# A scan's 64x64 chunk inverse: from full-width blocks to compressed blocks, two heads in one matmul

## The reference, cut to what matters

```
def step(S, inp):
    d_t, k_t, v_t, kk_t, a_t = inp[:5]
    sa = jnp.einsum("bhvk,bhk->bhv", S, -kk_t)
    S = (S * d_t[:, :, None, :] + sa[..., None] * (kk_t * a_t)[:, :, None, :]
         + v_t[..., None] * k_t[:, :, None, :])
    out = jnp.einsum("bhvk,bhk->bhv", S, inp[5]) if emit else None
    return S, out
```

## Time and profile before

| | us |
|---|---|
| median of 3 runs (2806.54 to 2811.82) | 2809.04 |
| the profiled execution, span | 2808.7 |
| time of the profiled execution outside its span, as far as the profile shows | none |
| scan, from about 1071 to 1757 | 686 |
| thirteen middle units of the scan (1179.5 to 1692) | 512.5 |

### The profile page before, as it was taken

One profiled execution on the slowest core, in us unless ns is written; L12 is line 12 of the kernel. 1 busy time (PEld: TensorE's weight loads), 2 busy tenths in 40 slices (PEclk: granted clock), 3 DMA queues, 4 the chain that ended last, 5 costly groups with the idle time before them and its releaser, 6 DMA issues. The chain is left out here.

```text
span 2808.7 us, 66348 instructions
## 1 busy us (share of the span) xinstructions
PE 2512.4 (89%) x28704; PEld 1935.4 (69%) x28704; DVE 1519.4 (54%) x2491; ACT 1099.4 (39%) x1771; POOL 735.1 (26%) x422
## 2 busy tenths in 40 slices
PE   7998899999889995888888887889999999898997
PEld 5776577777667784777777776768788655475666
DVE  4744589863652213556666663344542466525975
ACT  4633321152453433455545543334422344323133
POOL 2422301422212225555545551100000000032132
PEclk9999999999899996999999999989999999998998
DMA  4224344434335531111111100633522100044431
GB/s 159 83 68 135 128 135 124 122 105 162 116 125 183 201 122 59 43 43 55 38 54 54 32 15 26 240 129 103 159 79 86 57 0 1 11 173 139 137 109 68
DMA packets 90286, 272.63 MB, mean 97 GB/s; under 512 B 13584, under 2 KB 14608, under 8 KB 89872
## 3 DMA queue, kind: packets, MB, share of 16 engines
q1 hardware_dynamic: 73104, 229.25, 25.6%
q10 hardware_dynamic: 16896, 39.16, 4.0%
HBM read 203.01 MB, written 36.70 MB: 85 GB/s over the span
## 5 line engine op out<-in xcount | busy, mean ns | idle before, releaser
L375 PE MATMUL ps<-h_parts_conv,w_parts_one 128*128 128x512 f32 x3168 | 579.8, 343 | 16.9 <-DVE h_parts_conv L361 13.7
L375 PEld LDWEIGHTS ps<-h_parts_conv,w_parts_one 128*128 128x128 f32 x3168 | 492.4, 190 | 107.5 <-issue 24.1
L375 PE MATMUL ps<-scratch_scan 64*64 64x64 f32 (+1 forms) x16704 | 383.1, 234 | 96.2 <-issue 56.1
L375 PEld LDWEIGHTS ps<-scratch_scan 64*64 64x64 f32 x16704 | 345.9, 137 | 139.5 <-issue 105.8
L372 ACT ACTIVATE scratch_scan<-ps 128x384 f32<-128x384 f32 x560 | 238.4, 495 | 331.7 <-PE ps L375 180.3
L443 POOL TENSOR_TENSOR w_parts_one<-ring,w_parts_one 128x1024 fp32r<-128x1024 f32 x83 | 208.2, 2509 | 581.4 <-ACT w_parts_one L372 581.3
L375 PE MATMUL ps<-h_parts_attn,w_parts_rwkv_out 128*128 128x512 f32 (+1 forms) x1536 | 329.2, 373 | 4.6 <-DVE h_parts_attn L369 4.6
L375 PEld LDWEIGHTS ps<-h_parts_attn,w_parts_rwkv_out 128*128 128x128 f32 x1536 | 263.2, 189 | 64.0 <-issue 9.4
L443 POOL TENSOR_TENSOR w_parts_rwkv_out<-ring,w_parts_rwkv_out 128x1024 fp32r<-128x1024 f32 x31 | 74.6, 2409 | 812.5 <-ACT w_parts_rwkv_out L372 812.5
L369 DVE SCALAR_TENSOR_TENSOR scratch_conv<-scratch_conv,vec 128x512 f32<-128x512 f32 (+1 forms) x408 | 252.6, 691 | 0.2
L372 ACT ACTIVATE w_parts_rwkv_out<-ring 128x1024 fp32r<-128x1024 f32 x104 | 109.5, 1056 | 344.0 <-PE ps L375 325.8
(11 more groups left out here) (219 smaller groups left out, 3263.6 us busy)
## 6 DMA issues: line engine op xcount, KB each, us to landing
ring<-in_weights SPq DMA_DIRECT2D x311, 512.0 KB, 3.7
rwkv_spill<-scratch_conv ACTq DMA_DIRECT2D x64, 384.0 KB, 2.3
stream<-rwkv_spill SPq DMA_DIRECT2D x64, 384.0 KB, 3.6
scratch_conv<-scratch_conv SPq DMA_DIRECT2D x120, 103.1 KB, 2.2
scratch_conv<-scratch_conv SPq DMA_DIRECT2D x120, 67.4 KB, 2.0
x_spill<-stream ACTq DMA_DIRECT2D x16, 384.0 KB, 2.5
kept_gate<-scratch_attn ACTq DMA_DIRECT2D x64, 64.0 KB, 2.6
y_spill<-scratch_scan SPq DMA_DIRECT2D x8, 384.0 KB, 2.5
```

The source lines that it names most:

```text
L375: return nc.tensor.matmul(o, l, r, start=start, stop=stop)
```

## The change

P is now held compressed: before level n (block size b = 2^n) each row of a matrix keeps only the b columns of its own diagonal block, which stand in the first b of 64 columns of `PQ[(n - 1) % 2]`.
- There are six levels, `n` = 0 to 5. Level 0 needs no product with a P: `first_t` is six matmuls, each with a 128x128 stationary N (both heads and both halves) and a constant of four columns, `first_q` two matmuls with an identity. `first_inverse`, `p_start`, `p_diagonal` and the transposes PI are gone; a sixth transposition P6 of the whole inverse is there.
- `inv_t` is 12 matmuls (two heads side by side as 128 stationary columns, 64 rows), with 2b moving columns. `inv_q` is 12 matmuls (both heads as 128 stationary rows, 64 columns), with 2b moving columns from `TZ`, whose other half is zero.
- `t_copy` copies 12b elements for each half of the partitions.
- ScalarE writes the old P, times a row mask, into the two half blocks of the next size (`other_half`: two copies of 384 elements at n = 1 to 4, one at n = 0 and 5); VectorE adds Q to one of them (`inverse_update`, one operation of 384).
- The transposes P1 to P5 leave PSUM through VectorE, times a block mask (`turned_inverse`, two operations of 384 each); P6 goes through ScalarE (`full_turned`). The transposed k (`k_turned`) moves from VectorE to ScalarE.
- GpSimd masks N in one operation of 768 elements for each level.

TensorE's order of one phase becomes: T(1), WU, Q(1), WU, P2, BT, MR, T(2), NP, Q(2), MR, chain 1, P3, KT, chain 2, T(3), G, chain 3, Q(3), G, chain 4, AV, P4, VT, KS, chain 5, T(4), G, chain 6, Q(4), chain 7, RC, BO, P5, chain 8, T(5), AT, chain 9, `first_t` (for w1), Q(5), RS, chain 10, `first_q`, P6, outputs, P1 (for w1). On VectorE the new `inverse_update(w1, 0)` stands behind `cumulate`, and `turned_inverse(w1, 1)` is the last operation of the phase, behind `finish_out`, `normal_out` and `add_output`. On ScalarE `other_half(w2, n + 1)` stands right behind the copies that follow T(n). GpSimd's order is masks 2 and 3, `scaled_k`, mask 4, `bonus_add`, mask 5, `grown_k`, `grown_b`, `bonus_weights`, then masks 0 and 1 of w1.

```
-        NLV = 5
+        NLV = 6
...
-        T1, MT, NE = (take(NSTEP, CH) for _ in range(3))
+        MT, NE = (take(NSTEP, CH) for _ in range(2))
+        TZ, TZ0 = take(2, HALFC * CH), take(2, NSTEP)
...
+        def own(n, t):
+            b = inner(n)
+            return t.rearrange("p g (o b) -> p g o b", o=1).broadcast_to([P, NSTEP, max(CH // (2 * b), 1), b])
+
+        def half_of(n, side):
+            return PQ[n % 2].rearrange("p g (k s b) -> p g k s b", s=2, b=inner(n))[:, :, :, side, :]
...
+        def inverse_ready(engine, w, n):
+            if n == 1:
+                engine.wait_ge(*read_at("Q0", w, 0))
+            else:
+                engine.wait_ge(added, added_at(w, n - 1))
+            engine.wait_ge(halved, halved_at(w, n - 1))
...
-            def first_inverse(w):
...
+            def first_t(w):
+                pe.wait_ge(n_masked, masked_at(w, 0))
+                room_for(pe, "T0", w, 0)
+                first = fill_bank("T0", w, 0) * 512
+                o = PS[:, first:first + 2 * NSTEP].rearrange("p (x j y) -> p j y x", x=2, y=2)
+                ones = C("own_half").rearrange("p (y x) -> p y x", y=2)
+                for j in range(HALFC):
+                    last = mm(o[:, j, :, :], NT[0][:, 2 * j:2 * j + 2, :].rearrange("p h t -> p (h t)"), ones)
+                last.then_inc(*done_inc("T0", w, 0))
+
+            def first_q(w):
+                pe.wait_ge(*read_at("T0", w, 0))
...
+                for par in range(2):
+                    o = PS[HS[par], first:first + NSTEP].rearrange("p (j x) -> p x j", x=2)
+                    last = mm(o, C("ident2"), TZ0.rearrange("p x (j y) -> p y x j", y=2)[:, par])
+                last.then_inc(*done_inc("Q0", w, 0))
+
+            def inv_t(w, n):
+                pe.wait_ge(n_masked, masked_at(w, n))
+                inverse_ready(pe, w, n)
+                b = inner(n)
                 for j in range(HALFC):
                     for par in range(2):
...
+                        last = mm(PS[:, par * 512 + 2 * b * j:par * 512 + 2 * b * (j + 1)].rearrange("p (x b) -> p x b", x=2),
+                                  NT[n % 2][HS[par], 2 * j:2 * j + 2, :].rearrange("p h t -> p (h t)"), PQ[(n - 1) % 2][HS[par], 2 * j:2 * j + 2, 0:b])
+                        if j == HALFC - 1:
+                            last.then_inc(t_done, 1)
+
+            def inv_q(w, n):
+                pe.wait_ge(t_copied, 2 * product_at(w, n))
                 for e in range(2):
-                    pe.wait_ge(*read_at(f"P{lv}" if lv else "PI", w, e))
+                    pe.wait_ge(*read_at(f"P{n}", w, e))
...
                     for par in range(2):
-                        for h in range(2):
-                            last = mm(bank3(h)[HS[par], j, :], PT[w % 2][HS[h], 2 * j + par, :], T1[HS[h], 2 * j + par, :])
-                            if (j, par) == (HALFC - 1, 1):
-                                last.then_inc(q_done, 1)
+                        last = mm(PS[HS[par], 2 * b * j:2 * b * (j + 1)].rearrange("p (x b) -> p x b", x=2), PT[w % 2][:, 2 * j + par, :], t[:, par, j])
+                last.then_inc(q_done, 1)
...
+            def inverse_update(w, n):
...
+                    if n < NLV - 1:
+                        v.wait_ge(halved, halved_at(w, n))
+                        vtt(into, into, own(n, q), ALU.add).then_inc(added, 1)
                     else:
...
+                        stt(into[:, :, 0], PQ[(n - 1) % 2][:, :, 0:b], keep, q, ALU.mult, ALU.add).then_inc(added, 1)
...
+            def turned_inverse(w, n):
+                for e in range(2):
+                    v.wait_ge(*done_at(f"P{n}", w, e))
+                    vtt(blocks(n, PT[w % 2][:, half(e), :]), blocks(n, bank3(fill_bank(f"P{n}", w, e))), own_block(n)).then_inc(*read_inc(f"P{n}", w, e))
...
+            def t_copy(w, n):
+                a.wait_ge(t_done, 2 * product_at(w, n))
+                b = inner(n)
+                t = PS[:, 0:1024].rearrange("p (y z) -> p y z", y=2)[:, :, 0:NSTEP * b].rearrange("p y (j x b) -> p x y j b", x=2, b=b)
+                for h in range(2):
+                    act(TZ[HS[h], h, 0:NSTEP * b].rearrange("p (y j b) -> p y j b", y=2, b=b), t[HS[h], h], ACT.Copy).then_inc(t_copied, 1)
...
+            def other_half(w, n):
...
+                    before = own(n, PQ[(n - 1) % 2][:, :, 0:inner(n)])
+                    if n < NLV - 1:
+                        act(half_of(n, d), before, ACT.Copy, scale=keep).then_inc(halved, 1)
+                    act(into, before, ACT.Copy, scale=by).then_inc(halved, 1)
...
+            def off_blocks(w, n):
...
+                nc.gpsimd.tensor_tensor(NT[n % 2].rearrange("p (j s) t -> p j s t", s=2), XX[:, aa_plane(w), :, 0, :, :], level_mask(n),
+                                        ALU.mult).then_inc(n_masked, 1)
```

More of the change, by code:

```diff
@@ L83, in constants @@
     m = [((s // (2 * b) == t // (2 * b)) & (s // b != t // b))[:, :64] for b in (1, 2, 4, 8, 16, 32)]
-    m = [m[0] & (t < s)[:, :64], m[0] & (t > s)[:, :64], *m[1:]]
     put("inv_mask", np.concatenate(m, 1))
+    row, block = s[:, :1], np.arange(64)[None]
+    put("own_block", np.concatenate([row // 2 == block // 2, row // 4 == block // 4]
+                                    + [row // b == block[:, :64 // b] for b in (8, 16, 32)], 1))
+    put("even_rows", np.concatenate([row // b % 2 == 0 for b in (1, 2, 4, 8, 16, 32)], 1))
+    put("odd_rows", np.concatenate([row // b % 2 == 1 for b in (1, 2, 4, 8, 16, 32)], 1))
+    put("own_half", i // 64 == j[:, :4] // 2)
     w = []
@@ L2220, in setup @@
             def setup():
+                for t in (TZ, TZ0):
+                    nc.vector.memset(t, 0.0)
                 nc.vector.memset(CM, 1.0).then_inc(held_ready, 1)
@@ L2308, in mask_products @@
                     vtt(XXM[:, a:r + 1:r - a, 4 * jj:4 * jj + 4, h, :], o, m).then_inc(*read_inc("G", w, 2 * jj + h))
-            def inverse_update(w, lv):
-                for h in range(2):
-                    n = level(w, lv, h)
-                    v.wait_ge(q_done, n)
-                    if lv == 0:
-                        v.wait_ge(p_started, 2 * (w + 1))
-                    else:
-                        v.wait_ge(pq_ready, n - 2)
-                    pq = PQ[w % 2][:, h::2, :]
-                    vtt(pq, bank3(h), pq, ALU.add).then_inc(pq_ready, 1)
@@ L2353, in scan_vector @@
                 if two:
-                    inverse_update(w2, 0)
+                    inverse_update(w2, 1)
                 if one:
                     decayed_r(w1)
+                if two:
+                    turned_inverse(w2, 2)
+                if one:
                     decayed_a(w1)
@@ L2380, in scan_vector @@
                     next_state(w3, 4)
+                if two:
+                    turned_inverse(w2, 4)
+                if three:
                     next_state(w3, 5)
@@ L2396, in scan_vector @@
                         bonus_values(w1 // 2, e)
+                if two:
+                    turned_inverse(w2, 5)
                 if three:
@@ L2408, in scan_vector @@
                     cumulate(wc)
+                if one:
+                    inverse_update(w1, 0)
                 if fill_unit("RC", p - 1) is not None:
@@ L2415, in scan_vector @@
                         add_output(w3, e)
+                if one:
+                    turned_inverse(w1, 1)
             finish_out(NPAIR - 1)
@@ L2547, in scan_scalar @@
                     k_factor(wp)
[L2548 to L2549 removed]
+                T(2)
+                H(3)
+                if two:
+                    k_turned(w2, 0)
+                    k_turned(w2, 1)
                 if new_pair is not None:
                     kk_square(new_pair)
[L2552 removed]
+                T(3)
                 if prep:
@@ L2576, in scan_scalar @@
                     a_turned(w2, 1)
+                if one:
+                    other_half(w1, 0)
+                    first_t_copy(w1)
                 if read_pair is not None:
@@ L2580, in scan_scalar @@
                     out_inverse_root(read_pair)
-                turned(5)
-                if one:
-                    p_turned(0, w1, 0)
-                    p_turned(0, w1, 1)
+                if two:
+                    full_turned(w2, 0)
+                    full_turned(w2, 1)
                 if three and w3 % 2 == 0:
```

236 lines of the change are left out of this document (119 added, 117 removed), and 8 rows, old and new, of the table FILLS.

## The result

The changed kernel takes 2905.02 us (median of 4 runs, 2903.85 to 2910.79) against 2809.69 of the kernel before beside it: a ratio of 1.0342, 95% interval 1.0328 to 1.0357. It is slower by 3.4%, some 96 us; 57 were forecast. The profiled execution has a span of 2908.9 us and is the longest of the four.

The account below looks back on a forecast made before the run. TensorE's queue was taken to set the scan's pace, partly waiting for instructions. Loads 61, shape changes 44, instructions -70, waits -32, mask stalls 33, VectorE 9 and clock 12 gave +57 us: 2866 us, range 2795 to 2912.

Parts of the forecast that it names:

- shape changes: TensorE between array forms: 33 a unit instead of 12, 0.13 us each, +2.75 us a unit, 44 in all.
- TensorE's work: Scan's weight loads: T 0.61 us longer a block, `first_t` +1.31, `first_inverse` -0.70; +3.8 us a unit, 61 in all.
- rival 3: Q's column tiles of 128 rows load one after the other: +56 us, 2922; with the narrow-operand clock rival 0.14.
- Instruction supply: TensorE's queue in the scan: 544 fewer instructions a unit cut waits for them, -4.4 us a unit, 70 in all.
- Waits: TensorE's waits for VectorE's updates and the T copies in the scan: -2.0 of 2.8 us a unit, 32 in all.
- late VectorE: Odd phases, chain 10 to Q(1): VectorE's row of operations ends 1.3 us late, seven times, +9 us.
- The mask: `first_t` waits for GpSimd's level-0 mask in phases preparing a new pair: 4.7 us, seven times, +33 us.
- The clock: Behind each stall at `first_t` the granted clock falls to 0.50 for 3.4 us: 7 x 1.7 = +12 us.
- The scan's start and end: Scan's first and last units: priced like middle ones, per-unit terms times 16, as +3.8 us giving 61.
- 1 (no stall): At `first_t`: the late mask does not stall TensorE, so 33 and 12 go: +12 us, 2821; chance 0.17.
- 2 (faster): Scan: instruction supply was the bound and the extra work fits in what it frees: 2787 or 2765 us; chance 0.18.
- Rival 4: T and Q: narrow operands count as idle for the clock, +50 us, near 2920; with the column-tile rival 0.14.

Follow-up runs that it names:

- t64: The changed kernel with T as 24 products of 64x64 instead of 12 with 64x128 loads: 2862.18 us, ratio 1.0178 to the kernel before.
- early_wide: The changed kernel with GpSimd's level-0 mask ahead of `grown_k` and `grown_b`, and T always moving 32 columns of each head: 2850.76 us, ratio 1.0152.
- early_t64_q64: The changed kernel with the level-0 mask early, T and Q in 64x64 tiles, VectorE's update in two halves: 2843.68 us, ratio 1.0128.
- busy_wait: The changed kernel with 18 unused products of constants ahead of TensorE's wait for the level-0 mask, which stays late: 2881.78 us, ratio 1.0249.
- early_mask: The changed kernel with GpSimd's level-0 mask put ahead of `grown_k` and `grown_b`: 2853.48 us, ratio 1.0153.
- wide_moving: The changed kernel with T's moving operand always 32 columns of each head, the first b used: 2892.89 us, ratio 1.0281.
- early_t64: The changed kernel with the level-0 mask early and T in 64x64 tiles, b moving columns: 2830.95 us, ratio 1.0069.

## Why the prediction was right or wrong

Slower was right, and 2905 lies in the range (2795 to 2912), but 39 us above the number. Held against the 13 middle units, where nearly all the rows came from, the steps give +48 us (49 for loads, 36 for shape changes, -57 for instructions, -26 for old waits, +28 for six stalls, +8 for VectorE, +10 for the clock); measured +51.8. With what the runs show in place of each term the sum is 51 + 37 - 53 - 22 + 25 + 0 + 14 = 52 (the terms are taken up below; the shape changes are counted and priced from their steps). That the total came so near is in part luck: stalls and VectorE were 11 us too high, instructions, waits and clock 12 too low.

- **TensorE's work, right.** Forecast +3.8 us a unit. T64 shows 0.62 us a T block where I had 0.61. `first_t` takes 18.4 us in 13 units at nearly full clock (early_wide), 1.42 each, forecast 1.31; Q in column tiles 54.2 / 65 = 0.83 with some of it at half clock, like a 64x64 T block's 0.80. So 65 x 0.62 + 18.4 + 2.9 for `first_q`, less 13 x 0.8 for `first_inverse`, is +51 us, 3.9 a unit. Column tiles do load side by side: rival 3 is out.
- **Instruction supply and shape changes, right.** 94 packets in 13 units, 7.2 a unit (forecast 7.1; the earlier trace rows give 9.3). "Issue" time between two loads of one array form fell from 73.4 to 20.5 us in the 13 units: -53, forecast -57. That these gaps are waits for instructions is a reading: with fewer instructions they shrink (here) and with more they grow (t64, early_t64_q64), but no record names their cause. Changes of shape are 10 a unit before and 33 after (I had 12 and 33). From load to load one takes 0.20 us into the new forms and 0.22 (from 64x128) or 0.17 (from 128x64) out of them, against steps of 0.06 and 0.11 within a form: 0.11 to 0.14 net, where I took 0.13. 23 more a unit at 0.125 are 37 us in the 13 units. Whether they are worth removing at the price of more instructions is another question: in early_t64_q64 they were not.
- **Waits, right; VectorE, wrong.** VectorE and ScalarE held TensorE 34.0 us before and 12.2 after: -22 with what was to come at the phase's start, for which I had -26 and +8. The +9 for a late VectorE was wrong as a term: cumulate takes 1.75 us on the mean here, where the row that I used had 3.02, and the transposes' wait for VectorE is 2.2 us in all.
- **The mask, right.** Six stalls of 25.0 us, 4.2 each; I had 4.7. The units alternate between about 48 and 39 us (from one unit's first product of T(1) to the next unit's: 48.4, 39.7, 49.1, 39.4), forecast about 44 and 39. Of the extra 4 us in the long ones the larger part is the clock's: with the wait filled (busy_wait) the six long units take 44.1 to 47.1 us.
- **The clock, the term that was mis-sized.** I priced 1.7 us for a stall, 12 in all, from one fall of 3.4 us in the earlier trace rows. Behind the six long stalls it stays low for 6.8 to 13.7 us each (10.2 in the row above). busy_wait puts 26 us on it by the clock alone, 14 of them in the 13 units, where I had 10. I took the fall's length from one short gap. What a stall costs in all, waiting and clock, is not one figure either. Three pairs of runs differ by the early mask alone: in the first the loads of the scan wait 27 us less for masks and the program is 53 us shorter (early_mask), in the second 27 and 36 (wide_moving and early_wide), in the third 30 and 31 (t64 and early_t64). That is one to two times the stall's length. The Trainium skill ("TensorE: Matmul & The Clock Gate", HAM oscillation — how this bites in real kernels) tells of a kernel in which each wait for a DMA puts the engine back to the low level; here the waits are for GpSimd, and the trace agrees, 0.50 behind each of the six.
- **The scan's start and end, the step that failed.** I multiplied a middle unit by 16, which leaves 57 - 48 = 9 us for the units outside the 13. Ahead of the middle it was 105.7 us before and 128.5 after, behind it 61.2 and 67.1: +29. The two stretches of the kernel before, and the one behind the middle of the changed kernel:

```profile
1073.80:1179.50 105.70, 71.95 (x2050) 61.27 (x2050) 60.41 (x96) 45.55 (x88) 69.84 (x46) 0.77 0.15 47
1692.00:1753.20 61.20, 46.66 (x1438) 38.10 (x1438) 22.77 (x59) 21.11 (x48) 5.85 (x6) 0.94 0.08 27
```

```profile
1775.30:1842.40 67.10, 57.68 (x1204) 47.48 (x1204) 24.59 (x63) 21.54 (x49) 5.46 (x3) 0.82 0.08 26
```

It is not more waiting. Ahead of the middle the mask holds TensorE 13.3 us (6.2 before), once for 9.0, but VectorE holds it 8 us less, and all waits of the loads together are 48.9 us before and 50.2 after. It is the loads themselves: 61.3 and 82.9 us ahead, 38.1 and 47.5 behind, for fewer of them, at a clock of 0.70 instead of 0.77 and of 0.82 instead of 0.94. By these clocks 45 us more ran at the low level there, and at my price of 1.7 us for 3.4 that is an estimate of 23 us, most of the 29. My clock term has a single fall of 3.4 us for it: the rows of the middle, at full clock, do not show what the start and end do at a lower one. Why the clock is lower there is only in part known; behind the middle no mask is waited for.

- **Outside the scan, a term that was missing.** 19.7 us in the profile. 6 of them are this execution's own (it lies 5.8 above the median), 9 to 12 the width of the table; the rest, up to 5, stays open.
- **Rivals.** 1 (no stall) and 2 (faster) are out: both needed `first_t` in time. Rival 2's supply gain was real, 53 / 13 = 4.1 us a unit, and still smaller than the work. Rival 4 (narrow operands and the clock) is not out: the clock does rise with wide operands, and the time falls by 0 to 17 us. Most of the low clock in the 13 units sits behind the stalls, though: with the waits filled it is 0.98 instead of 0.93.

The three misses (+20 start and end, +14 outside without the execution's own 6, +4 middle) make the 38 us.

## What to carry to other kernels

Fewer columns in the moving operand buy nothing while weight loads set the pace; count loads by their columns first, and a product of two heads at once only if its load is not longer than the two it replaces. A stall of TensorE cost between one and two times its length here, by what the clock did behind it, and it went by moving one operation in another engine's order: ask of each new reader which of its producers stands behind something late. A unit from the middle of a pipeline says little of the stretches where it fills and drains, least of all where the clock is lower there: read those by themselves. And compare kernels whose buffers lie at the same addresses, or run one that differs in nothing else, before 0.3% is put down to a change.

## What the runs showed of the hardware

- Filling a wait with useless products made the program 0.9% faster: 18 products of 128x128 in 4.09 us, and the 28 loads behind them at 1.04 us instead of 1.77.
- A table of constants that is 136 bytes shorter, and the buffers behind it so much lower, costs 0.31% [0.16, 0.46] on the kernel before, and 0.3 to 0.4% on two changed ones; the median of the 128x512 matmuls of one projection is 392 ns in four profiles of the one layout and 396 or 397 in ten of the other.
- Loads of 64 rows and 128 columns in two row tiles take 1.42 us for 24, those of 128 rows and 64 columns in two column tiles 0.83 for 24, those of 64x64 in four tiles 0.80 for 48: the columns of a load count, and how many stand side by side, not its rows.
